# First out-projection of a fused two-block layer: a third k-turn of its second column group computed as seven block products

## The chip, the cores and the metric

One core of one Trainium2 chip runs the whole program. The metric is the device time of one execution in microseconds (us). The kernel before was run three times: 2097.71, 2097.87 and 2098.06 us.

## What is computed

The reference is a gated MLP mixer block followed by a second block (attention, mLSTM, gated feed-forward). The change touches one matrix product of it, the out-projection of the first block, whose result is added to the residual (abridged here, `sv` is the spatial mixing of 128-token chunks):

```
z = h @ w_in                                  # h: (256, 2048)
u, v, gate = jnp.split(z, 3, axis=-1)         # 4096 columns each
y = gelu(u) * sv(rmsnorm(gelu(v)))            # (256, 4096)
x = x + (y * silu(gate)) @ w_out              # w_out: (4096, 2048)   <- the product of the change
return rmsnorm(x, final_norm)                 # then the second block reads it
```

All is float32. The kernel gets there with float32r matmuls on halves: each operand is split into a high part and the rest, and a product is hi\*hi + hi\*lo + lo\*hi, three matmuls.

## The kernel before

**Items.** Weights come from DRAM as a stream of 512 KB chunks (128 partitions x 1024 values: two k-tiles of 128 rows, 512 columns). The unit of work is an item of the table `ITEMS`. For a plain item, SP loads the chunk into one of four `raw` buffers (L504), ScalarE (ACT) copies it to `w_hi` (`high_of_chunk`, L1014), VectorE (DVE) writes `w_lo = chunk - w_hi` (`low_of_chunk`, L1432), and TensorE (PE) runs 2 k-tiles x 2 token tiles x 3 = 12 matmuls of 512 columns into the PSUM tile `g` (`wide_chunk`, L653). `w_hi` and `w_lo` are rings of four: ACT starts item n when PE has finished item n-4 (`mm_done`), PE starts item n when DVE has counted `lo_ready` up to n+1. Each engine runs its own instructions in the order in which the loops emit them: in step n of a phase, ACT and DVE split item n+4 first and then do the side work of the step.

**Turns and groups.** The out-projection (phase `out1`) covers 2048 output columns in two groups of 1024. A turn is four k-tiles (512 rows of `w_out`) of one group. A plain turn is four plain items, C0 to C3, that is 48 matmuls. A turn "by products" computes the 2x2 block product with seven block multiplications instead of eight (Winograd's form): seven items P1 to P7 of 6 matmuls each (`wide_product`, L676 and L680), that is 42 matmuls. They need four tiles of sums of the left operand's rows and blocks (`sums_hi`, `sums_lo`, made once for a turn from `y_hi + y_lo`: `sums_of_rows`, L1519 to L1525, then `sums_high` on ACT, L1074, and `sums_low` on DVE, L1474), the four weight blocks in buffers of their own (`o_block`, loaded at L491), and four sums of weight blocks on DVE (`block_sums`, L1437). P1, P5, P6 and P7 gather in the PSUM tile `xs` over all turns by products of a group; P2, P3 and P4 go straight to `g`.

A step (a, b) of the table `WIDE_STEPS` interleaves a plain turn a with a turn b by products, eleven items in the order `MIXED`; (a, None) is a plain turn alone:

```
"out1": (((0, None), (1, None), (6, None), (2, 4), (3, 5), (7, None)),
         ((0, None), (1, None), (2, 4), (3, 5), (6, None), (7, None))),
MIXED = (1, "C0", 5, 7, "C1", 6, 3, "C2", 4, 2, "C3")
```

So each group of `out1` has 38 items. Items 38 to 45 are turns 0 and 1 of the second group, 46 to 56 the step (2, 4), 57 to 67 the step (3, 5), 68 to 75 turns 6 and 7. The sums of turns 4 and 5 are made in steps 1 and 4 (`SUMS_AT`), and serve both groups.

**The end of a group.** When P6 of the last turn by products is done, ACT copies P1's bank (L1112), and in that step and the next three DVE adds the gathered products to the residual `xt` (`add_products`, L1670 to L1680, two operations a step). When a half of `g` (two banks, 512 columns) has had its last matmul (`half_end`), DVE adds it to `xt` (`first_residual`, L1647) ahead of the split of that step, and counts `group_read` for that half; after the split it writes `xw = xt * final_norm` (`first_residual_gained`, L1658).

**What follows.** The next phase, `vv` (L556), opens the first half of `g` again: its first matmul waits for `group_read[0]`, that is for the residual addition of half 0 of the second group. Behind its first item PE transposes `xw` (`x_turned`, L604), which ACT (L1035) and DVE (L1480) split for the second block; behind its fourth item it transposes the last quarter.

Of the kernel before, what the change touches and what calls it, by code (L numbers as in the profile page):

```python
# [5 lines left out]
P = 128  # L6
S = 256
# [16 lines left out]
ACT = mybir.ActivationFunctionType  # L24
# [34 lines left out]
for _name, _w in (("a_norm", KD), ("norm1", KD), ("norm2", KD), ("b_s", GROUPS),  # L59
# [27 lines left out]
          ((0, None), (1, 3), (2, None)),  # L87
          ((0, 2), (1, 3))),
    "out1": (((0, None), (1, None), (6, None), (2, 4), (3, 5), (7, None)),
             ((0, None), (1, None), (2, 4), (3, 5), (6, None), (7, None))),  # L90
    "down": (((3, None), (4, None), (8, None), (9, None), (5, 0), (6, 1), (7, 2), (10, None)),
             ((3, 0), (7, None), (4, 1), (5, 2), (8, 6), (9, None), (10, None))),
    "gm0": (((0, 3), (1, 2)),),
# [2 lines left out]
}  # L96


SUM_TURNS = {"v": (3, 2), "out1": (4, 5), "down": (0, 1, 2, 6), "gm0": (3, 2), "out2": (1,)}


SUMS_AT = {"v": (4, 8), "out1": (1, 4), "down": (3, 6, 9, 64), "gm0": (-8, -5), "out2": (-7,)}

PLAIN = ("C0", "C1", "C2", "C3")
MIXED = (1, "C0", 5, 7, "C1", 6, 3, "C2", 4, 2, "C3")
# [3 lines left out]
ITEMS, FIRST_ITEM = [], {}  # L109
# [86 lines left out]
def sums_ahead(phase):  # L196

    return sum(len(turns) for name, turns in SUM_TURNS.items() if FIRST_ITEM[name] < FIRST_ITEM[phase])

# [63 lines left out]
def build(nc, x, x_tokens, stream, w_s, params, gain_rows, final_rows, gate_w, identity, consts, out):  # L263

    kib = 1024
# [8 lines left out]
    def sb(name, region, offset, shape, dt=F32):  # L274
        return nc.alloc_sbuf_tensor_at(name, shape, dt, offset=at[region] + int(offset))
# [13 lines left out]
    class Wide:  # L289
# [3 lines left out]
        def __init__(self, sb, name, blocks, hi, lo, rows, sums, u):  # L293
# [102 lines left out]
                     [("h", 12 * kib), ("h", 16 * kib), ("h", 20 * kib), ("y", 56 * kib)], ("h", 24 * kib), ("h", 28 * kib),  # L396
                     ("h", 24 * kib))
    out1_wide = Wide(sb, "o", [("mix", 0), ("mix", 4 * kib), ("x", 12 * kib), ("x", 4 * kib)],
                     [("h", 8 * kib), ("h", 12 * kib)], [("h", 24 * kib), ("h", 28 * kib)], ("h", 0), ("h", 16 * kib),
                     ("y", 88 * kib))  # L400
    wide = {"v": v_wide, "out1": out1_wide, "gm0": gm_wide, "gm1": gm_wide, "out2": out2_wide, "down": down_wide}
    u_sum = sb("u_sum", "mix", 4 * kib, [P, 4, S])

    par = sb("par", "small", 0, [P, N_PARAMS])
# [46 lines left out]
    sem = Sems()  # L451
    raw_full = [sem[f"raw_full{i}"] for i in range(RING)]
    block_full = [sem[f"block_full{b}"] for b in range(4)]
    hi_ready, lo_ready, mm_done = sem["hi_ready"], sem["lo_ready"], sem["mm_done"]
# [17 lines left out]
    with block:  # L472
# [68 lines left out]
        def _(pe):  # L541
# [117 lines left out]
            def wide_product(item, a_hi, a_lo, slot):  # L659

                p, i = item.product, sum_slot(item.phase, item.turn)
                sums = wide[item.phase]
                own = {1: 0, 5: 1, 6: 2, 7: 3}
                last = item.turn == last_by_products(item.phase, item.group)
                for j in range(2):
                    if p in (1, 2, 4):
                        kt = 4 * item.turn + j + (0 if p == 1 else 2)
                        t = 1 if p == 4 else 0
                        hi, lo = a_hi[:, kt, t * P:(t + 1) * P], a_lo[:, kt, t * P:(t + 1) * P]
                    else:  # L670
                        of = {5: 0, 6: 1, 7: 2, 3: 3}[p]
                        hi, lo = sums.sums_hi[i][:, of, j, :], sums.sums_lo[i][:, of, j, :]
                    for n, (a, w) in enumerate(((hi, w_hi), (hi, w_lo), (lo, w_hi))):
                        first = n == 0 and j == 0
                        if p in own:
                            ins = mm(XS[:, own[p], :], a, w[:, slot, half_chunk(j)],  # L676
                                     start=first and opens_own(item), stop=last and j == 1 and n == 2,
                                     skip_group_check=True)
                        else:
                            ins = mm(GG[:, RESULT_OF[p], :], a, w[:, slot, half_chunk(j)],  # L680
                                     start=first and opens(item, RESULT_OF[p]), stop=False, skip_group_check=True)
                return ins

            for n in range(items_of("v")):
                item = ITEMS[n]
# [58 lines left out]
            for n in range(items_of("out1")):  # L744
                at_item = FIRST_ITEM["out1"] + n
                item = ITEMS[at_item]
                pe.wait_ge(lo_ready, at_item + 1)
                if item.product:
                    if item.product == 1 and item.group == 0:

                        pe.wait_ge(sem["y_lo_ready"], GROUPS)
                        pe.wait_ge(sem["sv_read"], GROUPS)
                        pe.wait_ge(sem["sums_lo_ready"], sums_ahead("out1") + sum_slot("out1", item.turn) + 1)
                    if item.product == 1 and item.group == 1:

                        pe.wait_ge(sem["g_lo_ready"], 2)
                    ins = wide_product(item, y_hi, y_lo, at_item % RING)
                else:
                    if item.group == 0 and item.half == 0 and item.row % 2 == 0:
                        pe.wait_ge(sem["y_lo_ready"], item.turn + 1)  # L760
                    ins = wide_chunk(item, y_hi, y_lo, at_item % RING)
                ins.then_inc(mm_done, 1)
                if n == 4:
                    y_turned(GROUPS - 1)
                if n == out1_second + 1:
                    x_turned(0, xw[:, :, col_block(0)])
                if n == out1_second + 4:
                    x_turned(1, xw[:, :, col_block(1)])
# [107 lines left out]
            for c in range(96):  # L876
# [11 lines left out]
                n, step = divmod(c - HEAD_AT, 4)  # L888
# [17 lines left out]
            for p in range(2):  # L906
                gm, pa, pm = f"gm{p}", f"pa{p}", f"pm{p}"
                for n in range(items_of(gm)):
                    at_item = FIRST_ITEM[gm] + n
                    item = ITEMS[at_item]  # L910
# [25 lines left out]
            for n in range(items_of("out2")):  # L936
                at_item = FIRST_ITEM["out2"] + n
                item = ITEMS[at_item]
# [36 lines left out]
            for n in range(items_of("down")):  # L975
                at_item = FIRST_ITEM["down"] + n
                item = ITEMS[at_item]
# [15 lines left out]
        def _(act):  # L993
            activation = nc.scalar.activation
# [74 lines left out]
            def sums_high(phase, n):  # L1069

                if n - 2 in SUMS_AT[phase]:
                    i = SUMS_AT[phase].index(n - 2)
                    act.wait_ge(sem["sums_ready"], sums_ahead(phase) + i + 1)
                    activation(wide[phase].sums_hi[i][:], wide[phase].sums[:], ACT.Copy).then_inc(sem["sums_hi_ready"], 1)  # L1074

            def first_product(phase, n):

# [170 lines left out]
            for c in range(96):  # L1248
# [21 lines left out]
                if c % 8 == 7:  # L1270
                    n = c // 8
# [148 lines left out]
        def _(dve):  # L1420
# [51 lines left out]
            def low(to, of, hi, count, value, after):  # L1472
                dve.wait_ge(sem[count], value)
                return v.tensor_tensor(to, of, hi.bitcast(F32), ALU.subtract).then_inc(sem[after], 1)  # L1474
# [38 lines left out]
            def sums_of_rows(phase, n, a_hi, a_lo):  # L1513

                if n in SUMS_AT[phase]:
                    i = SUMS_AT[phase].index(n)
                    at_i = slice(4 * SUM_TURNS[phase][i], 4 * SUM_TURNS[phase][i] + 4)
                    rows, sums = wide[phase].rows, wide[phase].sums
                    link(v.tensor_tensor(rows[:], a_hi[:, at_i, :].bitcast(F32), a_lo[:, at_i, :].bitcast(F32), ALU.add))  # L1519
                    a11, a21 = rows[:, 0:2, 0:P], rows[:, 0:2, P:S]  # L1520
                    a12, a22 = rows[:, 2:4, 0:P], rows[:, 2:4, P:S]
                    v.tensor_tensor(sums[:, 2], a11, a21, ALU.subtract)
                    link(v.tensor_tensor(sums[:, 0], a21, a22, ALU.add))
                    link(v.tensor_tensor(sums[:, 1], sums[:, 0], a11, ALU.subtract))
                    v.tensor_tensor(sums[:, 3], a12, sums[:, 1], ALU.subtract).then_inc(sem["sums_ready"], 1)  # L1525

            def sums_low(phase, n):
                if n - 3 in SUMS_AT[phase]:
                    i = SUMS_AT[phase].index(n - 3)
                    low(wide[phase].sums_lo[i][:], wide[phase].sums[:], wide[phase].sums_hi[i][:], "sums_hi_ready",  # L1530
                        sums_ahead(phase) + i + 1, "sums_lo_ready")

            def own_products(phase, n):
# [150 lines left out]
            for n in range(items_of("out1")):  # L1684
                at_item = FIRST_ITEM["out1"] + n
                for q in range(4):
                    if at_item == half_end("out1", q // 2, q % 2):
                        first_residual(q)
                split("out1", n)
                for q in range(4):  # L1690
                    if at_item == half_end("out1", q // 2, q % 2):
                        first_residual_gained(q)
                if n == 0:

                    dve.wait_ge(mm_done, FIRST_ITEM["out1"])
                sums_low("out1", n)
                sums_of_rows("out1", n, y_hi, y_lo)
                if n == 5:
                    y_low(GROUPS - 1)
                if at_item == product_item("out1", 0, 5, 6) - 1:  # L1700
                    dve.wait_ge(sem["x_again"], 16)
                add_products("out1", at_item, xt)
                if n in (out1_second + 2, out1_second + 5):
                    gained_low(norm_mid, (n - out1_second - 2) // 3, 0, TR)
# [427 lines left out]
```

## Time and profile before

| | |
|---|---|
| time, median of three runs | 2097.87 us |
| the profiled execution's own time | 2097.71 us |
| its span, first to last instruction | 2095.9 us (1.8 us lie around it) |
| TensorE busy | 2089.8 us, 100% |
| weight loads of TensorE (beside the matmuls) | 1750.1 us, 84% |
| VectorE busy | 1506.6 us, 72% |
| ScalarE busy | 1112.4 us, 53% |
| granted TensorE clock, mean | 1.000 (2.4 GHz) |
| DMA | 404.40 MB, mean 193 GB/s |
| `out1`, second group: from its first product to the first matmul of `vv` | 650.73 to 713.34 us |

Busy shares are means over the whole program. A matmul of 512 columns is listed with some 0.39 us, but matmuls are pipelined: the distance from one start to the next is what counts. Idle time of an engine that is not waited for costs nothing.

### The profile page before, as it was taken

Reading aid. Unit: us, or ns where it says so; the run is one execution under the profiler, and the core shown is the slowest. Engines: PE = TensorE matmul, PEld = TensorE weight load, DVE = VectorE, ACT = ScalarE, POOL = GpSimd, SP = SyncE. Lnnn points to the kernel's source line nnn. Section 1 sums busy time; section 2 is a strip of 40 time slices with the busy share of each in tenths; the row PEclk is TensorE's granted clock in tenths of the full one; section 3 lists DMA queues with packets and bytes.
Section 4 is the critical chain, followed back from the end, with each engine's and each line's share of the span. In section 5 each row is a group of like instructions: output and inputs, shape, how many; then the busy total and the mean of one; then the engine's idle time right before and its main releaser. Section 6 shows DMA issues by size and latency. Waiting matters only on the chain.

```text
span 2095.9 us, 25218 instructions
## 1 busy us (share of the span) xinstructions
PE 2089.8 (100%) x10000; PEld 1750.1 (84%) x10000; DVE 1506.6 (72%) x1702; ACT 1112.4 (53%) x1314; POOL 17.5 (1%) x17
## 2 busy tenths in 40 slices
PE   9999999999999999999999999999999999999999
PEld 7888888888888887888888888888888888888887
DVE  7987656655787754665669678867777777779986
ACT  6765444444456544555455454555555555555553
POOL 0000000000000000100000000000000000000000
PEclk9999999999999999999999999999999999999999
DMA  8665555555764555544465656556556566556663
GB/s 337 210 200 175 198 187 187 194 187 189 272 214 157 194 194 171 177 155 153 150 210 181 221 169 208 167 185 192 187 185 195 183 192 190 181 181 232 224 203 133
DMA packets 111957, 404.40 MB, mean 193 GB/s; under 512 B 12512, under 2 KB 13280, under 8 KB 111328
## 3 DMA queue, kind: packets, MB, share of 16 engines
q1 hardware_dynamic: 109440, 394.66, 57.1%
q10 hardware_dynamic: 2400, 8.14, 1.0%
q8 instruction: 79, 1.29, 0.3%
q14 instruction: 38, 0.31, 0.0%
HBM read 400.65 MB, written 2.10 MB: 192 GB/s over the span
## 4 chain that ended last, share of the span: by engine, by line
PE 96%; DVE 3%; ACT 1%; DMA 0%; issue 0%; ACTq 0%; DVEq 0%
PE g L556 37%; PE g L653 23%; PE xs L581 8%; PE g L581 8%; PE xs L676 5%; PE xs L585 4%; PE g L585 4%; PE g L680 4%; DVE w_lo L1432 1%; PE xs L604 1%; PE xs L713 1%; ACT w_hi L1014 0%; PE xs L833 0%; DMA xf<-in_x 0%; PE xs L830 0%
## 5 line engine op out<-in xcount | busy, mean ns | idle before, releaser
L1432 DVE TENSOR_TENSOR w_lo<-raw,w_hi 128x1024 fp32r<-128x1024 f32 x659 | 803.4, 1223 | 492.6 <-ACT w_hi L1014 486.9
L1014 ACT ACTIVATE w_hi<-raw 128x1024 fp32r<-128x1024 f32 x659 | 697.4, 1059 | 756.6 <-PE g L556 411.7
L556 PE MATMUL g<-w_hi,mid_both 128*128 128x512 f32 x1024 | 326.7, 394 | 0.0
L556 PE MATMUL g<-w_hi,in_both 128*128 128x512 f32 x1024 | 318.8, 390 | 0.1
L556 PEld LDWEIGHTS g<-w_hi,in_both 128*128 128x128 f32 x1024 | 192.2, 188 | 40.3 <-DVE v_all L1564 0.5
L556 PEld LDWEIGHTS g<-w_hi,mid_both 128*128 128x128 f32 x1024 | 192.3, 188 | 39.6
L556 PE MATMUL g<-w_lo,mid_both 128*128 128x512 f32 x512 | 199.4, 389 | 0.0
L556 PE MATMUL g<-w_lo,in_both 128*128 128x512 f32 x512 | 199.2, 389 | 0.0
L581 PE MATMUL g<-mlp_both,w_hi 128*128 128x512 f32 x704 | 176.8, 393 | 0.0
L581 PE MATMUL xs<-mlp_both,w_hi 128*128 128x512 f32 x704 | 176.3, 392 | 0.0
L581 PEld LDWEIGHTS g<-mlp_both,w_hi 128*128 128x128 f32 x704 | 126.5, 189 | 22.8
L581 PEld LDWEIGHTS xs<-mlp_both,w_hi 128*128 128x128 f32 x704 | 126.6, 189 | 22.6
L653 PE MATMUL g<-w_hi,in_both 128*128 128x512 f32 x352 | 112.6, 390 | 1.3 <-DVE w_lo L1500 1.0
L556 PEld LDWEIGHTS g<-w_lo,in_both 128*128 128x128 f32 x512 | 96.1, 188 | 19.7
L556 PEld LDWEIGHTS g<-w_lo,mid_both 128*128 128x128 f32 x512 | 96.3, 188 | 19.1
L585 PEld LDWEIGHTS g<-mlp_both,w_lo 128*128 128x128 f32 x704 | 96.2, 190 | 7.0
L585 PEld LDWEIGHTS xs<-mlp_both,w_lo 128*128 128x128 f32 x704 | 96.0, 190 | 6.9
L585 PE MATMUL g<-mlp_both,w_lo 128*128 128x256 f32 x704 | 98.3, 282 | 0.0
L585 PE MATMUL xs<-mlp_both,w_lo 128*128 128x256 f32 x704 | 98.2, 282 | 0.0
L653 PE MATMUL g<-w_hi,f_hi 128*128 128x512 f32 x240 | 93.7, 390 | 0.2
L653 PE MATMUL g<-w_hi,f_lo 128*128 128x512 f32 x240 | 93.4, 389 | 0.0
L653 PE MATMUL g<-w_lo,f_hi 128*128 128x512 f32 x240 | 93.4, 389 | 0.0
(404 smaller groups left out, 3044.3 us busy)
## 6 DMA issues: line engine op xcount, KB each, us to landing
raw<-in_stream SPq DMA_DIRECT2D x659, 512.0 KB, 3.5
d_block<-in_stream SPq DMA_DIRECT2D x28, 512.0 KB, 4.6
o_block<-in_stream SPq DMA_DIRECT2D x24, 512.0 KB, 4.7
v_block<-in_stream SPq DMA_DIRECT2D x20, 512.0 KB, 4.4
gm_block<-in_stream SPq DMA_DIRECT2D x12, 512.0 KB, 5.1
x_first<-in_x_tokens ACTq DMA_DIRECT2D x2, 1024.0 KB, 6.8
gain_row<-in_gain_rows SPq DMA_DIRECT2D x8, 256.0 KB, 3.5
xt<-in_x_tokens ACTq DMA_DIRECT2D x1, 2048.0 KB, 8.0
```

Of the source, the lines that this page charges most:

```text
L556: ins = mm(G[buf][:, t, :], a[:, kt, at_t], w[:, slot, j * COLS:(j + 1) * COLS], start=(kt == 0 and n == 0), stop=(last and j == ROWS_PER_ ...
L581: mm(UP[buf][:, b, :, :], w_hi[:, slot, j * COLS + b * P:j * COLS + (b + 1) * P], a_both[:, :, kt, :], start=(kt == 0), stop=False, skip_g ...
L585: ins = mm(UP[buf][:, b, 0, :], w_lo[:, slot, j * COLS + b * P:j * COLS + (b + 1) * P], a_both[:, 0, kt, :], start=False, stop=(last and j ...
L604: ins = turn(TR[:, b, t * P:(t + 1) * P], of[:, t, b * P:(b + 1) * P], ident[:])
L653: ins = mm(GG[:, bank, :], a[:, kt, t * P:(t + 1) * P], w[:, slot, half_chunk(j)], start=n == 0 and opens(item, bank), stop=ended and n == ...
L676: ins = mm(XS[:, own[p], :], a, w[:, slot, half_chunk(j)], start=first and opens_own(item), stop=last and j == 1 and n == 2, skip_group_ch ...
L680: ins = mm(GG[:, RESULT_OF[p], :], a, w[:, slot, half_chunk(j)], start=first and opens(item, RESULT_OF[p]), stop=False, skip_group_check=True)
L713: ins = mm(SV[:, t, :], w[:, t, :], a[:, t, :], start=(n == 0), stop=(n == 2))
L1014: activation(w_hi[:, n % RING, :], of[:], ACT.Copy).then_inc(hi_ready, 1)
L1432: v.tensor_tensor(w_lo[:, n % RING, :], of, w_hi[:, n % RING, :].bitcast(F32), ALU.subtract).then_inc(lo_ready, 1)
```

## The change

Turn 6 of the second group is computed by products, interleaved with turn 7, as the last step of the group. Its sums of rows are made in step 46, when PE has finished turns 0 and 1 of the second group and nobody reads those two turns' rows of `y_hi` and `y_lo` again; the rows, the sums and their two halves are put in that place. In the first group turn 6 stays plain. The changed `out1` has 79 items: 68 to 78 are the step (7, 6).

```diff
-             ((0, None), (1, None), (2, 4), (3, 5), (6, None), (7, None))),
+             ((0, None), (1, None), (2, 4), (3, 5), (7, 6))),
...
-SUM_TURNS = {"v": (3, 2), "out1": (4, 5), "down": (0, 1, 2, 6), "gm0": (3, 2), "out2": (1,)}
-
-
-SUMS_AT = {"v": (4, 8), "out1": (1, 4), "down": (3, 6, 9, 64), "gm0": (-8, -5), "out2": (-7,)}
+SUM_TURNS = {"v": (3, 2), "out1": (4, 5, 6), "down": (0, 1, 2, 6), "gm0": (3, 2), "out2": (1,)}
+
+
+SUMS_AT = {"v": (4, 8), "out1": (1, 4, 46), "down": (3, 6, 9, 64), "gm0": (-8, -5), "out2": (-7,)}
...
-                     [("h", 8 * kib), ("h", 12 * kib)], [("h", 24 * kib), ("h", 28 * kib)], ("h", 0), ("h", 16 * kib),
-                     ("y", 88 * kib))
+                     [("h", 8 * kib), ("h", 12 * kib), ("y", 0)], [("h", 24 * kib), ("h", 28 * kib), ("y", 32 * kib)],
+                     ("h", 0), ("h", 16 * kib), ("y", 88 * kib))
+
+    out1_last_rows = sb("o_last_rows", "y", 4 * kib, [P, 4, S])
+    out1_last_sums = sb("o_last_sums", "y", 36 * kib, [P, 4, 2, P])
...
+    def made_from(phase, i):
+
+        if (phase, i) == ("out1", 2):
+            return out1_last_rows, out1_last_sums
+        return wide[phase].rows, wide[phase].sums
...
+                    if item.product == 1 and item.turn == 6:
+                        pe.wait_ge(sem["sums_lo_ready"], sums_ahead("out1") + 3)
...
+                if n == SUMS_AT["out1"][2]:
+
+                    dve.wait_ge(mm_done, FIRST_ITEM["out1"] + n)
                 sums_low("out1", n)
                 sums_of_rows("out1", n, y_hi, y_lo)
```

(`sums_high`, `sums_of_rows` and `sums_low` take their tiles from `made_from` now.)

**Order on VectorE at the end of the second group.** `o_u` are the gathered products, `xt` the residual, `g` the PSUM tile, `xw` what the next phase transposes. Before:

```order
L1679 TENSOR_TENSOR o_u_195<-xs,o_u_195 128x512
L1680 TENSOR_TENSOR xt<-xt,o_u_195 128x512 [waits dve_step]
L1432 TENSOR_TENSOR w_lo<-raw,w_hi 128x1024 [waits dve_step,hi_ready]
L1432 TENSOR_TENSOR w_lo<-raw,w_hi 128x1024 [waits hi_ready] x6
L1647 TENSOR_TENSOR xt<-g,xt 128x2x512 [waits mm_done]
L1432 TENSOR_TENSOR w_lo<-raw,w_hi 128x1024 [waits hi_ready,group_read0]
L1658 TENSOR_TENSOR xw<-xt,final_row 128x2x512
```

The same place after the change:

```order
L1682 TENSOR_TENSOR o_u_196<-xs,o_u_195 128x512 [waits mm_done,p1_ready]
L1683 TENSOR_TENSOR xt<-xt,o_u_195 128x512 [waits dve_step]
L1444 TENSOR_TENSOR w_lo<-raw,w_hi 128x1024 [waits hi_ready]
L1685 TENSOR_TENSOR o_u_197<-xs,o_u_196 128x512
L1686 TENSOR_TENSOR xt<-xt,o_u_197 128x512 [waits dve_step]
L1444 TENSOR_TENSOR w_lo<-raw,w_hi 128x1024 [waits hi_ready]
L1688 TENSOR_TENSOR o_u_196<-xs,o_u_196 128x512
L1689 TENSOR_TENSOR xt<-xt,o_u_196 128x512 [waits dve_step]
L1444 TENSOR_TENSOR w_lo<-raw,w_hi 128x1024 [waits hi_ready]
L1691 TENSOR_TENSOR o_u_197<-xs,o_u_197 128x512
L1692 TENSOR_TENSOR xt<-xt,o_u_197 128x512 [waits dve_step]
L1659 TENSOR_TENSOR xt<-g,xt 128x2x512 [waits dve_step,mm_done]
```

The eight additions of gathered products now stand right before the first residual addition; the seven splits that lay between them have gone ahead or behind.

**Order on VectorE at item 46**, in the step (2, 4) of the second group. Before:

```order
L1432 TENSOR_TENSOR w_lo<-raw,w_hi 128x1024 [waits hi_ready]
L1432 TENSOR_TENSOR w_lo<-o_block_185,w_hi 128x1024 [waits hi_ready]
L1437 TENSOR_TENSOR o_block_185<-o_block_186,o_block_185 128x1024 [waits lo_ready,block_full3]
L1432 TENSOR_TENSOR w_lo<-o_block_184,w_hi 128x1024 [waits hi_ready]
L1432 TENSOR_TENSOR w_lo<-raw,w_hi 128x1024 [waits hi_ready]
```

After:

```order
L1444 TENSOR_TENSOR w_lo<-raw,w_hi 128x1024 [waits hi_ready]
L1531 TENSOR_TENSOR o_last_rows<-y_hi,y_lo 128x1024 [waits mm_done]
L1534 TENSOR_TENSOR o_last_sums<-o_last_rows 128x256 [waits dve_step]
L1535 TENSOR_TENSOR o_last_sums<-o_last_rows 128x256
L1536 TENSOR_TENSOR o_last_sums<-o_last_sums,o_last_rows 128x256 [waits dve_step]
L1537 TENSOR_TENSOR o_last_sums<-o_last_rows,o_last_sums 128x256 [waits dve_step]
L1444 TENSOR_TENSOR w_lo<-o_block_185,w_hi 128x1024 [waits hi_ready]
L1449 TENSOR_TENSOR o_block_185<-o_block_186,o_block_185 128x1024 [waits lo_ready,block_full3]
L1444 TENSOR_TENSOR w_lo<-o_block_184,w_hi 128x1024 [waits hi_ready]
L1444 TENSOR_TENSOR w_lo<-raw,w_hi 128x1024 [waits hi_ready]
L1486 TENSOR_TENSOR o_sums_lo_192<-o_last_sums,o_sums_hi_189 128x1024 [waits sums_hi_ready]
```

Five operations have come between the splits of items 50 and 51, and one, `o_sums_lo`, behind the split of item 53.

## Rows read from the trace of the kernel before

**Rows 1.** The page: busy time of TensorE, and the chain's shares by engine.
```profile
PE 2089.8 (100%) x10000; PEld 1750.1 (84%) x10000; DVE 1506.6 (72%) x1702; ACT 1112.4 (53%) x1314; POOL 17.5 (1%) x17
...
PE 96%; DVE 3%; ACT 1%; DMA 0%; issue 0%; ACTq 0%; DVEq 0%
```

**Rows 2.** Waits of TensorE: waited for, us in total, times, longest us.
```profile
PE xs L609 <- DVE ones L1487: 1.1, 1, 1.1
...
PEld g L556 <- DVE v_all L1564: 0.5, 1, 0.5
```

**Rows 3.** Windows: us, busy (count) of PE, PEld, DVE, ACT, POOL; PEclk, DMA share, GB/s.
```profile
0.00:4.00 4.00, 2.95 (x14) 2.95 (x15) 0.18 (x2) 1.49 (x2) 0.20 (x4) 1.00 0.51 141
...
651.00:692.00 41.00, 41.00 (x182) 33.96 (x181) 36.38 (x35) 23.77 (x24) 0.00 (x0) 1.00 0.46 153
```

**Rows 4.** Timeline of PE, second group: start us, us, instruction.
```profile
661.66 0.39 PE L680 MATMUL g<-w_hi,o_sums_hi 128*128 128x512 f32 x1
...
671.18 0.39 PE L676 MATMUL xs<-w_hi,y_hi 128*128 128x512 f32 x1
...
682.06 0.39 PE L680 MATMUL g<-w_hi,o_sums_hi 128*128 128x512 f32 x1
...
691.58 0.39 PE L653 MATMUL g<-w_hi,y_hi 128*128 128x512 f32 x1
...
713.34 0.39 PE L556 MATMUL g<-w_hi,mid_both 128*128 128x512 f32 x1
```

**Rows 5.** Timeline of DVE: first sums of rows of `out1`, and the split behind.
```profile
549.95 1.22 DVE L1519 TENSOR_TENSOR o_rows<-y_hi,y_lo 128x1024 f32<-128x1024 f32 x1
...
552.80 1.22 DVE L1432 TENSOR_TENSOR w_lo<-raw,w_hi 128x1024 fp32r<-128x1024 f32 x1
```

**Rows 6.** Timeline of DVE, step (2, 4) of the second group: items 50, 51.
```profile
654.02 1.22 DVE L1432 TENSOR_TENSOR w_lo<-raw,w_hi 128x1024 fp32r<-128x1024 f32 x1
656.21 1.23 DVE L1432 TENSOR_TENSOR w_lo<-o_block,w_hi 128x1024 fp32r<-128x1024 f32 x1 [0.97 <-ACT w_hi L1014]
657.54 1.23 DVE L1437 TENSOR_TENSOR o_block<-o_block,o_block 128x1024 f32<-128x1024 f32 x1
```

**Rows 7.** Timeline of DVE, end of step (3, 5) of the second group.
```profile
682.05 2.58 DVE L1432 TENSOR_TENSOR w_lo<-o_block,w_hi 128x1024 fp32r<-128x1024 f32 x2 [0.61 <-ACT w_hi L1014]
684.56 0.68 DVE L1670 TENSOR_TENSOR o_u<-xs,o_u 128x512 f32<-128x512 f32 x1
685.27 0.69 DVE L1671 TENSOR_TENSOR xt<-xt,o_u 128x512 f32<-128x512 f32 x1
685.88 1.22 DVE L1432 TENSOR_TENSOR w_lo<-raw,w_hi 128x1024 fp32r<-128x1024 f32 x1
...
692.66 0.69 DVE L1680 TENSOR_TENSOR xt<-xt,o_u 128x512 f32<-128x512 f32 x1
693.50 3.50 DVE L1432 TENSOR_TENSOR w_lo<-raw,w_hi 128x1024 fp32r<-128x1024 f32 x3
```

**Rows 8.** Timeline of DVE, end of the second group: residual addition, split, `xw`.
```profile
708.10 1.22 DVE L1647 TENSOR_TENSOR xt<-g,xt 128x1024 f32<-128x1024 f32 x1 [0.34 <-PE g L653]
709.36 1.23 DVE L1432 TENSOR_TENSOR w_lo<-raw,w_hi 128x1024 fp32r<-128x1024 f32 x1
710.50 1.22 DVE L1658 TENSOR_TENSOR xw<-xt,final_row 128x1024 f32<-128x1024 f32 x1
```

**Rows 9.** Timeline of DVE and PE where phase `v` ends and `ug` begins.
```profile
175.10 1.28 DVE L1564 TENSOR_TENSOR v_all<-g,v_u 128x512 f32<-128x512 f32 x2
...
176.44 0.50 PE L556 MATMUL g<-w_hi,in_both 128*128 128x512 f32 x1
```

**Rows 10.** Block loads between 640 and 715 us: their issue, their landing, the use.
```profile
662.91 1.69 SPq L491 DMA_DIRECT2D o_block<-in_stream  x2
...
670.73 1.22 DVE L1437 TENSOR_TENSOR o_block<-o_block,o_block 128x1024 f32<-128x1024 f32 x1
...
DMA to landing us min/median/max: 3.2/4.0/5.2
```

More of the change, by code:

```diff
@@ L1073, in sums_high @@
                     act.wait_ge(sem["sums_ready"], sums_ahead(phase) + i + 1)
-                    activation(wide[phase].sums_hi[i][:], wide[phase].sums[:], ACT.Copy).then_inc(sem["sums_hi_ready"], 1)
+                    activation(wide[phase].sums_hi[i][:], made_from(phase, i)[1][:], ACT.Copy).then_inc(sem["sums_hi_ready"], 1)
             def first_product(phase, n):
@@ L1517, in sums_of_rows @@
                     at_i = slice(4 * SUM_TURNS[phase][i], 4 * SUM_TURNS[phase][i] + 4)
-                    rows, sums = wide[phase].rows, wide[phase].sums
+                    rows, sums = made_from(phase, i)
                     link(v.tensor_tensor(rows[:], a_hi[:, at_i, :].bitcast(F32), a_lo[:, at_i, :].bitcast(F32), ALU.add))
@@ L1529, in sums_low @@
                     i = SUMS_AT[phase].index(n - 3)
-                    low(wide[phase].sums_lo[i][:], wide[phase].sums[:], wide[phase].sums_hi[i][:], "sums_hi_ready",
+                    low(wide[phase].sums_lo[i][:], made_from(phase, i)[1][:], wide[phase].sums_hi[i][:], "sums_hi_ready",
                         sums_ahead(phase) + i + 1, "sums_lo_ready")
```

## The prediction

> **What bounds the kernel now.** I read the page first. TensorE is busy for 2089.8 of 2095.9 us, and 96% of the chain that ended last is its own work [rows 1]. So the question for each edit is whether it takes matmuls away or makes TensorE wait. The view of waits shows that TensorE hardly waits at all: its longest wait is 1.1 us, at the very start, and where one phase hands PSUM to the next the longest is 0.5 us, from `v` to `ug` [rows 2]. The windows come third: in 651 to 692 us, the two mixed steps of the second group, TensorE is busy all the time at granted clock 1.00 (the 2.4 GHz level), but VectorE is busy 36.38 of 41 us [rows 3]. VectorE is thus the engine with the least room just where the change puts work. Last, the timelines of both engines, from which all prices below come.
>
> The rhythm of TensorE: the step (3, 5) runs from 671.18 to 691.58 us [rows 4]. It has 4 plain items of 12 matmuls and 7 products of 6, 90 in all, so a matmul takes 20.40/90 = 0.2267 us, a product 1.36 us and a plain item 2.72 us.
>
> **Term 1, matmuls.** Turn 6 goes from 48 matmuls to 42. Six fewer at 0.2267 us: **-1.36 us**, all of it on TensorE's path. (The Trainium skill, "TensorE: Matmul & The Clock Gate", Part 1, gives 215.7 ns from start to start for 512 columns at the full clock; an estimate from that page is -1.29 us. The trace's 226.7 ns is 5% longer, and the trace is used.)
>
> **Term 2, the sums of rows in step 46.** VectorE has finished the split of item 50 at 654.02 + 1.14 = 655.16 us (1.14 us is the distance of operations back to back, 709.36 to 710.50 [rows 8]). The five operations take 2.85 us, from 549.95 to 552.80 us [rows 5], so they end at 658.01. The idle 0.97 us before item 51's split [rows 6] covers a third of that; the rest pushes what is queued behind on VectorE. Item 51 (P6) is split from 658.01 instead of 656.21; its block sum follows 1.33 us later as before (656.21 to 657.54 [rows 6]), at 659.34; item 52 (P3) is split from 660.48 and its operation ends at 661.70. TensorE wants P3 at 661.66 [rows 4]. It starts 0.06 us after the VectorE operation that it waits for ends (176.38 to 176.44 [rows 9]), so at 661.76, and the first matmul after a wait is listed with 0.50 us instead of 0.39 [rows 9], 0.11 us more. **+0.2 us**. Item 53 is ready by 662.9 and wanted at 663.3, and then comes `o_sums_lo`, 1.14 us more on VectorE before item 54, which is ready by 665.1 and wanted at 666.0; the idle time that VectorE has before item 57 takes up the rest. The bounds: 0, if the restart costs nothing, and 0.6 us, if each of the five operations and their own waits takes a tenth longer.
>
> The new wait on VectorE in this step (`mm_done` up to item 45) costs nothing: item 50's `w_hi`, which VectorE has just used, needed item 46 to be finished. ScalarE gets one copy of 1024 columns more for `sums_hi` and three more splits in all; it is busy 23.77 of 41 us [rows 3], and its copy holds up only item 53's split, which VectorE reaches three operations later. TensorE's own new wait, for the third `sums_lo`, is met at about 664 us and asked for at 691.6.
>
> On SP nothing is added in bytes: four chunks of turn 6 go to block buffers instead of `raw`. But the block loads for the step (3, 5) wait for splits that are now up to 2.2 us late. The one with the least room was issued at 662.91 and was used at 670.73; landing took 5.2 us at most [rows 10]. Issued at 665.1 it lands by 670.3. Cover: 0.4 us at the worst landing, and then still the 1 us or so by which VectorE is ahead of P7. Nothing.
>
> **Term 3, the end of the group.** Here lies the price of the change. In the kernel before, step (3, 5) is the last one with products, and the eight additions of the gathered products fall among VectorE's splits behind it, with turns 6 and 7 (21.76 us of TensorE work) as cover. In the changed kernel the step (7, 6) is last, only five items follow its P6, and half 0 of `g` ends with P2, the last but one. The order shows that the residual addition of half 0 stands right behind the eight additions on VectorE, and the first matmul of `vv` waits for it.
>
> What the queue costs can be read off the step (3, 5), for VectorE does the same there in the same order. P6 ends and P3 starts at 682.06 [rows 4]. VectorE is then busy without a gap: two splits from 682.05, two additions at 684.56 and 685.27, a split at 685.88, and so on in a period of 2.46 us (1.14 for the split and 1.32 for the pair), four times; the last addition starts at 692.66 and ends at 693.35 [rows 7]. What follows starts at 693.50, a gap of 0.15 us. From P6's end this is 11.44 us. In the changed kernel the residual addition stands there: 1.22 us [rows 8], then 0.06 us to TensorE, 0.11 us for the restart [rows 9]. Sum: 11.44 + 1.22 + 0.06 + 0.11 = 12.83 us. TensorE has 3 products and 2 plain items left after P6: 682.06 to 691.58, 9.52 us [rows 4]. So it waits 12.83 - 9.52 = **+3.3 us**.
>
> All of it is on the path: nothing else is ready for TensorE. The bounds: the nearest row of a wait at such a handover is 0.5 us [rows 2], but there VectorE has half as many additions; above, 3.8 us, if the reads of PSUM meet each other's banks and each step takes 0.1 us more. I take 3.3, since it is read off the same sequence.
>
> What is late next: `xw` for the first transposition. It is ready 3.62 us after the residual addition starts (708.10 to 710.50 + 1.22 [rows 8]), 2.4 us after it ends, and the first item of `vv` takes 2.72 us. Covered, by 0.2 us with the early weight load. The splits of the first three items of `vv` come in time, being done before or right behind the addition; later ones have the whole wait as extra lead.
>
> **The sum.** -1.36 + 0.2 + 3.3 = +2.1 us. The profiled execution took 2097.71 us, so it would take 2099.8 us; the median is 0.16 us above it, so **2100.0 us**. The change gives TensorE 0.06% less to do and lets it stand idle for more than twice that. A difference under 0.2% (4.2 us, so 2093.7 to 2102.1) is about what a measurement of this kernel can't tell from no change.
>
> **Rivals.**
> *A, the end wait stays hidden.* VectorE's lead would be larger than I make it, or the addition of half 0 comes early enough. For it: the handover from `v` to `ug` costs only 0.5 us [rows 2], and there too a step with products is last. Against it: `v` has no additions to a residual, half the work; here the trace shows VectorE without a gap for 11 us. It would give 2097.87 - 1.36 + 0.2 = 2096.7 us, plus up to 0.5.
> *B, the clock falls (slower).* TensorE stands still for 3.2 us, three times its longest wait so far, at the start of `vv`. If the granted clock then drops to its 1.2 GHz level, a matmul of 512 columns takes 512/1.2 GHz = 0.427 us instead of 0.227, 0.20 us more. The other side of the 0.2% begins 2.1 us above my forecast, so it decides from 11 such matmuls on. One item of `vv` (12 matmuls) would give 2102.4, two items 2104.8 us; I put it at 2103.5. For it: nothing in this trace, which has no wait of that length. Against it: the clock stays 1.00 through the first 4 us, where TensorE is busy for 2.95 us only [rows 3]. The Trainium skill, "TensorE: Matmul & The Clock Gate", Part 1, says that the clock gate falls back to 1.2 GHz once TensorE has stood idle and opens again only after it has been busy for a while; by that rule the price of B would be due. No row here bears it out or refutes it at this length.
> *C, a block load or the sums come late in the middle.* The cover of 0.4 us at the worst landing is thin, and the sums could cost more. Then up to 1 us more waits show near 661 or 676 us: 2101.0 us.
> That the change doesn't do what it says can be left out: the order of TensorE has six matmuls fewer.
>
> **How the numbers follow.** Forecast 0.74 (its own range, -1.36 plus 0 to 0.6 plus 2.9 to 3.8: 2099.4 to 2100.9), A 0.10, B 0.10, C 0.06. A and C lie within 0.2%, so the chance of "same" is 0.74 + 0.10 + 0.06 less 0.01 for a result that I can't name: 0.89. B lies outside for nine tenths: 0.10 with that. Faster by over 0.2% would need 4 us less, three times the matmuls taken away: 0.01. The range reaches down to A (2096.7) and up to the edge of B: 2096.6 to 2102.2 leaves out most of B alone.
>
> **What would show it.** In the changed profile: TensorE busy for 1.4 us less in `out1`; one wait of its weight load or matmul L566 on VectorE's `xt` L1659 of about 3.2 us, at 712 us; a wait of 0.1 to 0.2 us on `w_lo` at 661.7; VectorE without a gap from about 702.5 to 717 us; granted clock 1.00 in 712 to 724. The prediction is wrong if the wait at 712 us is under 2 us, if a wait over 0.6 us stands in the step (2, 4) or (3, 5), or if the clock shows under 1.00 behind the wait.

## The result and the profile after

| | before | changed |
|---|---|---|
| median of 18 runs each | 2097.86 us | 2101.42 us |
| lowest and highest | 2097.60, 2098.21 | 2099.79, 2102.99 |
| the profiled execution, its span | 2097.71, 2095.9 | 2101.66, 2099.7 |

The ratio is 1.0017, 95% interval 1.0010 to 1.0023. The change costs 3.6 us, 0.17%: inside the 0.2% (the interval ends just above it, at 0.23%) and inside the range, 1.4 us above the forecast of 2100.0 us. One thing in the table was not there before: the runs of the kernel before lie within 0.6 us, those of the changed one within 3.2 us. Three of the 18 took 2099.8 to 2100.2 us, twelve 2101.0 to 2101.7, three 2102.1 to 2103.0.

The page of the changed kernel, against [rows 1]: six matmuls fewer, TensorE still on 96% of the chain, but listed as busy for 1.6 us more, though it has less to do.

```profile
PE 2091.4 (100%) x9994; PEld 1750.8 (83%) x9994; DVE 1518.0 (72%) x1715; ACT 1116.6 (53%) x1318; POOL 17.5 (1%) x17
...
PE 96%; DVE 3%; ACT 1%; DMA 1%; issue 0%; ACTq 0%; DVEq 0%
```

The view of TensorE's waits, against [rows 2], has a new line at its head: the first matmul of `vv` waits 3.0 us for the residual addition of half 0. The second row is from the same view of the weight loads in 640 to 740 us; it is the wait for P3's `w_lo` in the step (2, 4).

```profile
PE g L566 <- DVE xt L1659: 3.0, 1, 3.0
...
PEld g L690 <- DVE w_lo L1444: 0.3, 1, 0.3
```

VectorE's timeline at the end of the group. It corresponds to [rows 7] with 20.96 us added, and the residual addition (L1659) stands where the split at 693.50 stood:

```profile
703.01 2.58 DVE L1444 TENSOR_TENSOR w_lo<-o_block,w_hi 128x1024 fp32r<-128x1024 f32 x2 [0.61 <-ACT w_hi L1026]
705.51 0.68 DVE L1682 TENSOR_TENSOR o_u<-xs,o_u 128x512 f32<-128x512 f32 x1
706.23 0.69 DVE L1683 TENSOR_TENSOR xt<-xt,o_u 128x512 f32<-128x512 f32 x1
706.84 1.22 DVE L1444 TENSOR_TENSOR w_lo<-raw,w_hi 128x1024 fp32r<-128x1024 f32 x1
...
713.62 0.69 DVE L1692 TENSOR_TENSOR xt<-xt,o_u 128x512 f32<-128x512 f32 x1
714.46 1.23 DVE L1659 TENSOR_TENSOR xt<-g,xt 128x1024 f32<-128x1024 f32 x1
```

TensorE's timeline across the wait: last matmul of `out1`, first item of `vv`, first transposition.

```profile
703.02 0.39 PE L690 MATMUL g<-w_hi,o_sums_hi 128*128 128x512 f32 x1
...
712.31 0.39 PE L663 MATMUL g<-w_hi,y_lo 128*128 128x512 f32 x1
715.74 0.50 PE L566 MATMUL g<-w_hi,mid_both 128*128 128x512 f32 x1 [3.04 <-DVE xt L1659]
716.07 0.39 PE L566 MATMUL g<-w_lo,mid_both 128*128 128x512 f32 x1
716.30 0.99 PE L566 MATMUL g<-w_hi,mid_both 128*128 128x512 f32 x2
717.10 0.63 PE L566 MATMUL g<-w_lo,mid_both 128*128 128x512 f32 x1
717.52 1.05 PE L566 MATMUL g<-w_hi,mid_both 128*128 128x512 f32 x2
718.38 0.63 PE L566 MATMUL g<-w_lo,mid_both 128*128 128x512 f32 x1
718.80 1.05 PE L566 MATMUL g<-w_hi,mid_both 128*128 128x512 f32 x2
719.66 0.45 PE L566 MATMUL g<-w_lo,mid_both 128*128 128x512 f32 x1
719.95 0.40 PE L566 MATMUL g<-w_hi,mid_both 128*128 128x512 f32 x1
720.19 1.03 PE L614 MATMUL xs<-ident,xw 128*128 128x128 f32 x8
```

Two things are to be seen. From 712.31 to 715.74 TensorE starts nothing: 3.43 us instead of 0.23. And soon behind it the matmuls do not follow each other at 0.227 us but at some 0.43 us (717.10 to 718.38 is three of them, 1.28 us), until 719.66. The windows say why: the granted clock, 1.00 in the windows before, is 0.57 on average in 716 to 720 us.

```profile
708.00:712.00 4.00, 4.00 (x19) 3.33 (x18) 3.93 (x7) 2.54 (x3) 0.00 (x0) 1.00 0.55 156
712.00:716.00 4.00, 0.96 (x5) 0.50 (x4) 3.79 (x5) 1.06 (x1) 0.00 (x0) 1.00 0.62 238
716.00:720.00 4.00, 4.00 (x12) 3.09 (x12) 3.97 (x4) 0.00 (x0) 0.00 (x0) 0.57 0.43 131
720.00:724.00 4.00, 4.00 (x23) 3.41 (x22) 3.77 (x6) 2.51 (x5) 0.00 (x0) 1.00 0.54 150
```

Windows of half a microsecond show when it fell: not during the standstill, in which it stays at 1.00, but within 0.8 us after TensorE's restart at 715.74. The first two or three matmuls still follow each other at full speed.

```profile
715.50:716.00 0.50, 0.26 (x1) 0.26 (x2) 0.47 (x2) 0.00 (x0) 0.00 (x0) 1.00 0.09 33
716.00:716.50 0.50, 0.50 (x3) 0.41 (x3) 0.50 (x1) 0.00 (x0) 0.00 (x0) 0.86 0.00 0
716.50:717.00 0.50, 0.50 (x2) 0.41 (x2) 0.50 (x2) 0.00 (x0) 0.00 (x0) 0.50 0.00 0
```

The first item of `vv` takes 4.45 us (715.74 to 720.19); at full clock it would be 12 x 0.227 and 0.11 for the restart, 2.83 us. The low clock costs 1.6 us here.

### The profile page after: what moved, and what is told of

It reads as the page before. It is cut to its first block, busy times and chain, and to the rows that moved or that the text cites. A ratio compares the mean times of both kernels' runs of the same rounds, so it can differ in the third digit from the quotient of the medians.

```text
span 2099.7 us, 25230 instructions
## 1 busy us (share of the span) xinstructions
PE 2091.4 (100%) x9994; PEld 1750.8 (83%) x9994; DVE 1518.0 (72%) x1715; ACT 1116.6 (53%) x1318; POOL 17.5 (1%) x17
## 4 chain that ended last, share of the span: by engine, by line
PE 96%; DVE 3%; ACT 1%; DMA 1%; issue 0%; ACTq 0%; DVEq 0%
PE g L566 37%; PE g L663 22%; PE xs L591 8%; PE g L591 8%; PE xs L686 6%; PE xs L595 4%; PE g L595 4%; PE g L690 4%; PE xs L614 1%; DVE w_lo L1444 1%; PE xs L723 1%; PE xs L845 0%; ACT w_hi L1026 0%; DMA raw<-in_stream 0%; PE xs L842 0%
```

## The experiments

The theory has two parts. *Queue*: TensorE's wait is the eight additions that stand ahead of the residual addition on VectorE. *Clock*: the rest, some 1.5 us, is the granted clock, which falls because TensorE has stood still. The medians of the kernel before in the three groups of runs were 2098.08 (e1 to e4), 2097.84 (e5 to e7) and 2097.87 us (e8, e9).

### e1: fill the wait

```diff
+            pe.wait_ge(sem["p1_ready"], own_ahead("vv"))
+            for _ in range(14):
+                mm(XS[:, 0, :], y_hi[:, 8, 0:P], y_hi[:, 8:10, :], start=True, stop=True, skip_group_check=True)
```

> The changed kernel with 14 matmuls of 512 columns more on TensorE between the last item of out1 and the first of vv, into the bank of P1 that has been copied out; their result is used by nobody. They take 14 x 0.2267 = 3.17 us, about the wait that the changed kernel has there (3.0 to 3.3 us), and need nothing from VectorE. Theory (queue and clock): the wait is VectorE's and stays as long, so the fillers hide in it; but TensorE is never idle for long, the granted clock stays 1.00 in every run, and the 1.5 us behind the wait go away: 2099.9 us, with the runs within 0.3 us of each other as in the kernel before. Rival (refill): the slow matmuls behind the wait come from something other than the clock, such as the queues refilling or memory traffic of the late splits: they stay, 2101.4 us or more. Second rival: fillers are simply added to the path: 2101.4 + 3.2 = 2104.6 us.

Measured: 2099.79 us, 1.6 us less than the changed kernel, though TensorE has 14 matmuls more. (The two were run in different groups; against the kernel before of its own group the one costs 1.7 us, the other 3.6.) All 11 runs had a granted clock of 1.000 and ten of them lie within 0.5 us; one took 2100.75. The timeline of TensorE shows the fillers and full speed behind them:

```profile
712.29 3.33 PE L783 MATMUL xs<-y_hi 128*128 128x512 f32 x14
715.49 0.50 PE L566 MATMUL g<-w_hi,mid_both 128*128 128x512 f32 x1
715.83 0.40 PE L566 MATMUL g<-w_lo,mid_both 128*128 128x512 f32 x1
716.06 0.62 PE L566 MATMUL g<-w_hi,mid_both 128*128 128x512 f32 x2
716.52 0.39 PE L566 MATMUL g<-w_lo,mid_both 128*128 128x512 f32 x1
```

So the slow matmuls are the clock's, and here the clock fell because TensorE stood idle. What is left above the kernel before, 1.7 us in this group, is near what the sum of the prediction gives without the clock, 2.1; of the 0.4 us between them, the kernel before moved by 0.2 from group to group, and the rest is not explained.

### e2 and e3: one and two pairs of additions less

In `add_products`, for the second group of `out1` alone, the last pair (e2) or the last two pairs (e3) are left out, so that the last 512 columns lack them.

> The changed kernel without the last pair of additions of gathered products in the second group (the last 512 columns of the second token tile lack them). Theory (queue): each pair stands on VectorE ahead of the residual addition with 1.32 us, so TensorE's wait at the start of vv falls from 3.3 to 2.0 us. If a wait of 2 us leaves the clock alone: 2099.9 - 1.3 = 2098.6 us; if the clock falls all the same, up to 1.5 us more, 2100.1 us. Rival: the residual addition waits for P2 or the banks, not for the queue: no change, 2101.4 us.

> The changed kernel without the last two pairs of additions of gathered products in the second group (the last 512 columns lack them in both token tiles). Theory (queue): the wait falls by another 1.32 us to 0.7 us, the clock stays 1.00 in all runs: 2097.3 us, with all runs within 0.3 us. Rival (not the queue): no change, 2101.4 us.

Measured: 2098.29 and 2097.11 us, the clock 1.000 in all 22 runs. The waits of the first matmul of `vv`, in e2:

```profile
PE g L566 <- DVE xt L1659: 1.5, 1, 1.5
```

and in e3:

```profile
PE g L566 <- DVE xt L1659: 0.3, 1, 0.3
```

From 3.0 to 1.5 to 0.3 us: each pair is worth 1.2 to 1.6 us of waiting, 1.4 on average (1.32 forecast). The times follow: 2099.8 (e1, no clock loss), 2098.3, 2097.1. The wait is the queue's, and the rival (the ends of P2 and C3, the banks) falls.

### e4: the sums of rows alone

```diff
-             ((0, None), (1, None), (2, 4), (3, 5), (7, 6))),
+             ((0, None), (1, None), (2, 4), (3, 5), (6, None), (7, None))),
```

(on the changed kernel, so that the third set of sums is made and nobody reads it)

> The kernel before with the third set of sums of rows made in step 46 (five operations on VectorE, one copy on ScalarE, one sums_lo), which nobody reads; turn 6 stays plain, 76 items. Theory: only the step (2, 4) of the second group feels it, +0.2 us, 2098.1 us, with a wait of 0.1 to 0.2 us for P3's w_lo. Rival (the sums are the cost): the new VectorE work delays splits and block sums through both mixed steps, +1 us or more, 2099 us.

Measured: 2097.81 us, 0.3 us *below* the kernel before of the same group (2098.08, runs from 2097.61 to 2098.78), which says only that 0.2 us can't be resolved by time. The trace has the wait, the same as the changed kernel's:

```profile
PEld g L690 <- DVE w_lo L1444: 0.3, 1, 0.3
```

The rival (1 us or more from the sums) falls.

### e5: the place alone

```diff
-             ((0, None), (1, None), (2, 4), (3, 5), (6, None), (7, None))),
+             ((0, None), (1, None), (6, None), (7, None), (2, 4), (3, 5))),
...
-            out1_second = product_item("out1", 1, 4, 1) - FIRST_ITEM["out1"] - 8
+            out1_second = 38
```

(on the kernel before; the second edit in its three places)

> The kernel before with its second group in another order: turns 0, 1, 6, 7 plain, then the steps (2, 4) and (3, 5) last. No third turn by products, no new sums, the same 10000 matmuls; the transpositions of the first half stay where they were, at items 38 + 1 and 38 + 4. Theory (place): what costs is that a step with products is last in the group, since the eight additions then stand right before the residual addition of half 0: a wait of 3.3 us at the start of vv and about 1.5 us of low clock behind it: 2097.9 + 3.3 + 1.5 = 2102.7 us. Rival (work): what costs is the third turn's own VectorE work (a third set of splits, block sums and sums): then the order alone changes nothing, 2097.9 us.

Measured: 2102.67 us, 4.8 us above the kernel before of its group, with no third turn at all. The wait is there, with the same length as in the changed kernel:

```profile
PE g L556 <- DVE xt L1647: 3.0, 1, 3.0
```

Nine of ten runs showed a clock under 1.000 and took 2102.4 to 2103.9; the tenth, at 1.000, took 2101.03, 3.2 us above the kernel before. So the price is the place of a step with products, not the work of the third turn.

### e6 and e7: half 0 first

The last step in another order; e7 in addition moves the third pair of additions behind the next split and the first transposition of `vv` from behind its first to behind its second item.

```diff
+MIXED_HALF0 = (1, "C0", 5, 7, "C1", 6, 2, 4, "C2", 3, "C3")
...
+                          else MIXED_HALF0 if (_name, _turn) == ("out1", 7) else MIXED):
...
-                if c == 0:
+                if c == 1:
                     x_turned(2, xw[:, :, col_block(2)])
...
-                    if after == 2:
+                    if after == (3 if (phase, g) == ("out1", 1) else 2):
```

(the last two edits are in e7 alone; in both, VectorE waits for the second pair before it goes on, since the residual addition reads what it wrote)

> The changed kernel with the last step in the order P1, C0, P5, P7, C1, P6, P2, P4, C2, P3, C3, so that half 0 of g has its last matmul with P4, three items before the end, and the residual addition of half 0 stands ahead of the third and fourth pair on VectorE. Theory (queue): from P6's end the residual addition now ends at 2.5 + 1.3 + 2.5 + 1.2 = 7.5 us, before TensorE needs half 0 at 9.5, so the wait of 3.3 us at the first matmul of vv is gone. But the fourth pair now ends at 13.6 us and the first transposition, which waits for it since it writes the same banks, is due at 12.2: a new wait of 1.4 us there, at L614. The clock stays 1.00. Sum: 2097.9 - 1.4 + 0.2 + 1.5 = 2098.2 us. Rival: the wait at vv is set by P2's and C3's ends and not by the queue: it stays, 2101 us.

> The same order of the last step, the third pair of additions moved behind the next split (together with the fourth), and the first transposition of vv moved from behind its first item to behind its second. Theory (queue): now neither the first matmul of vv nor the transposition waits: 2097.9 - 1.4 + 0.2 = 2096.7 us, faster than both kernels by what the six matmuls bring. Cover that is thin: the low half of the transposed quarter must be ready at the fifth item of vv, 21.2 us after P6's end, and VectorE gets to it at 21.1 us; up to 0.3 us of wait there, 2097.0 us. Rival: the other places take it back (a wait at the fifth item of 1 us or more): 2098 us.

Measured: e6 2098.30 us, e7 2096.77 us, the clock 1.000 in all runs. In e6 the wait at the first matmul of `vv` is gone and one at the transposition has come, 1.6 us against 1.4 forecast. The profile names no releaser for it ("issue"); that it is the fourth pair is read from the times, since VectorE ends that pair at 716.55 and the transposition starts at 716.71:

```profile
PE xs L616 <- issue: 1.6, 1, 1.6
```

In e7 TensorE goes from `out1` into `vv` without a break. VectorE ends the residual addition of half 0 at 710.38, before TensorE wants the half:

```profile
708.44 0.69 DVE L1688 TENSOR_TENSOR xt<-xt,o_u 128x512 f32<-128x512 f32 x1
709.16 1.22 DVE L1661 TENSOR_TENSOR xt<-g,xt 128x1024 f32<-128x1024 f32 x1
```

and TensorE:

```profile
712.06 0.39 PE L665 MATMUL g<-w_hi,y_lo 128*128 128x512 f32 x1
712.28 0.39 PE L568 MATMUL g<-w_hi,mid_both 128*128 128x512 f32 x1
```

e7 computes what the reference asks for and beats both kernels: its 11 runs lie from 2096.47 to 2097.18 us, the 26 runs of the kernel before in the same group from 2097.56 to 2098.13. The gain is 1.1 us, 0.05%; the interval of the ratio, 0.9986 to 1.0004, doesn't exclude 1, but no run of the one overlaps a run of the other. That is near the 1.4 us of the six matmuls less the 0.2 us of the sums.

### e8 and e9: the clock and the length of the standstill

e8 has 5 fillers instead of e1's 14. e9 has two more VectorE operations of 512 columns ahead of the residual addition, in the second group of `out1` alone:

```diff
+                            link(v.tensor_tensor(u_d[:], u_b[:], p1[:], ALU.add))
+                            link(v.tensor_tensor(u_d[:], u_d[:], p1[:], ALU.add))
```

> The changed kernel with only 5 filler matmuls (1.1 us) at the start of TensorE's wait before vv: the wait on VectorE ends when it ended before, but TensorE stands still for only some 2.1 us of it. Theory (clock): stretches of 1.9 us left the clock at 1.00 in the runs before, so 2.1 us does as well: 2099.9 us, as with 14 fillers. Rival (the slow matmuls depend on something else in the last microseconds before vv, or on the length of the whole wait): 2101.4 us, with clock under 1.00.

> The changed kernel with one more pair of VectorE operations of 512 columns (into a tile that nobody reads, each waited for) between the last pair of additions and the residual addition. Theory (queue): the wait grows by the pair, 1.4 to 1.7 us, to about 4.8 us, and the time with it: 2101.4 + 1.6 = 2103.0 us if the clock costs what it cost in the changed kernel; every run then shows the clock under 1.00, where three of 18 did not at 3.3 us. Rival (clock): the longer the wait, the longer the low clock, up to 1 us more: 2104 us.

Measured: e8 2101.24 us. The theory's number was 2099.9, so it missed: the clock was under 1.000 in 7 of 11 runs (2101.0 to 2101.8 us), and in four it stayed (2100.0 to 2100.5). In its profiled run the standstill had this length:

```profile
715.80 0.50 PE L566 MATMUL g<-w_hi,mid_both 128*128 128x512 f32 x1 [1.91 <-DVE xt L1662]
```

(The "1.9 us" of e8's expectation are counted from the start of the last matmul to the start of the next. As the profile lists waits, those stretches are the 1.5 us of e2 and the 1.6 us of e6, so e8's 1.9 us is longer than any of them.)

e9: 2104.02 us, all 7 runs at 0.998. The theory's number was 2103.0, and it missed too: the rival, a longer stretch of low clock (2104 us), is what came. The wait is 1.45 us longer than in the changed kernel, and the clock's share grew by 0.8 us; the whole first item of `vv` ran slowly, 5.23 us from 717.33 to 722.56 instead of 2.83, a loss of 2.4 us. Here the clock did fall during the wait: it is 0.66 in 715.5 to 716.0 us and 0.50 from there to the restart.

```profile
717.33 0.80 PE L566 MATMUL g<-w_hi,mid_both 128*128 128x512 f32 x1 [4.49 <-DVE xt L1659]
...
722.56 1.03 PE L614 MATMUL xs<-ident,xw 128*128 128x128 f32 x8
```

1.45 and 0.8 us are 2.25; the two profiled executions differ by 2.30 us (2103.96 and 2101.66).

## Why the prediction came out as it did

**Term 1** held: 9994 matmuls instead of 10000, and the item rhythm is unchanged. From the last P3's start to the end of the group (703.02 to 712.31 + 0.23) are 9.52 us, as in the prediction. From the P3 of the step (2, 4) to the end of the group TensorE takes 50.46 us (from 662.08) instead of 51.68 (661.66 to 713.34): 1.22 us less, the 1.36 but for the slow restart that term 2 counts.

**Term 2** held in the trace, while the times can't resolve it (e4): P3 started 0.30 us after its predecessor instead of 0.23, and with the slow restart that makes 0.2 us. The covers named for it (block loads, `o_sums_lo`, the new `mm_done` wait) all held: no other new wait of TensorE stands between 640 and 712 us.

**Term 3** held to a tenth of a microsecond: 12.83 us were forecast from P6's end to the first matmul of `vv` at full rhythm; measured are 715.74 - 703.02 = 12.72 and the 0.11 of the restart. (The lower bound of 2.9 us that the range gives this term has no row behind it; the wait of 3.2 us and the restart are 3.3.) The way to that number is worth keeping: not from durations added up, but from a stretch of the same trace in which VectorE already did the same work in the same order.

**The sum** left a term out, and this is the step that failed: the likeliest case, and the sum with it, put the clock at nothing. Rival B was not a rival but a part of that case: 15 of 18 runs showed the clock lower, and the prediction's own sign of being wrong, a clock under 1.00 behind the wait, is there. B's mechanism stood in the text, its chance (0.10) was far too small and its size too large: I priced it at 12 to 24 slow matmuls, and in the profiled execution it was about 8, 1.6 us. 2100.0 + 1.6 = 2101.6 us; the median is 2101.42. It lies above the forecast's own range (2099.4 to 2100.9) and inside the wide one (2096.6 to 2102.2), and that is in part luck: with the whole item slow, as in e9, it would have been 2102.4. The three runs in which the clock stayed at 1.000 took 2099.8 to 2100.2 us: the forecast itself.

What was wrong about B was the argument against it from the first 4 us of the trace: that stretch has a wait of 1.1 us, and says nothing about one of 3.2. The runs showed in its place a clock of 0.57 in 716 to 720 us behind 3.0 us of standstill, and 1.000 in all 11 runs of e1, whose fillers took the standstill's place. The Trainium skill's rule of the falling clock ("TensorE: Matmul & The Clock Gate", Part 1), that it falls back once TensorE has stood idle, was the only statement at hand about this; the runs agree with its direction. They do not agree with it on how long the standstill must be: in e8 the clock fell in 7 of 11 runs at 1.9 us, earlier than by that rule, and the measurement decides.

**Rivals A and C** fell: the wait was there in full, and nothing came late in the middle.

## What to carry to other kernels

When a step is moved to the end of a phase, look at what the next phase's first instruction waits for, and count everything that now stands ahead of that releaser in its engine's queue: here the change saved 1.4 us and paid 3.3 for a place in a queue, and 1.6 for the clock. The cure was order, not less work: finish first the part that is wanted first. And price a new standstill of TensorE with the slow matmuls behind it: here they cost half of the wait again (1.6 us after 3.0), and in some runs of e8 they came after 1.9 us already.

## What the runs showed of the hardware

How often the clock fell, with the length of the standstill as each kernel's one profiled run lists it, all at the start of `vv` (e6's stands an item later, ahead of the transposition): after 0.3 (e3), 1.5 (e2) and 1.6 us (e6) it stayed at 1.000 in all 33 runs; after 1.9 us (e8, with five filler matmuls before it) it was lower in 7 of 11; after 3.0 us in 15 of 18 and in 9 of 10 (e5); after 4.5 us in 7 of 7. The loss was 1.6 us after 3.0 us and 2.4 us after 4.5 us. I had expected e8 to be safe. Between 1.6 and 1.9 us the kernels differ in more than the length (e8 has the fillers), so no bound is shown there.

When it fell differed too: in the profiled runs of the changed kernel, of e5 and of e8 the clock was still at 1.00 all through the standstill and fell within 1.2 us after the restart, so that the first matmuls ran at full speed; in e9 it fell inside the standstill. A wait's own window can thus show a clock of 1.00 though the price comes behind it.

What decides between two runs of the same kernel is not shown. It makes the spread of such a kernel larger: 3.2 us against the 0.6 of the kernel before in the same group of runs (which in the group of e1 to e4 spread over 1.2 us itself).
